# Eight more turns by blocks and a way through DRAM, in place of 64 TensorE transposes; the first such turn of the first feed-forward three units later

## What is computed

```python
# first block
x = x + 0.5 * swiglu(rmsnorm(x, ffn1_norm), ffn1_w_gu, ffn1_w_down)      # f1
h = rmsnorm(x, mix_norm)                                                # rows turned: "x"
z = h @ w_in                                   # u, v, c_q, c_kv, k_rope, q_m, gates
y_a = spatial_gating(gelu(u), gelu(v), ...)                              # turned: "a"
y_b = mla(c_q, c_kv, k_rope, positions, ...)
q = rmsnorm(q_m heads); kv = rmsnorm(mem) @ w_kv; k = rmsnorm(k heads)   # turned: "qm", "mk"
y_c = softmax(q k^T * 128 ** -0.5) v           # 4 heads of 128; turned: "c"
x = x + (g0 * (y_a @ w_a) + g1 * (y_b @ w_b) + g2 * (y_c @ w_c)) @ w_out
x = x + 0.5 * swiglu(rmsnorm(x, ffn2_norm), ...)                         # f2
# second block: gate_b, gate_c, hv = split(h2 @ conv_w_in)
u2 = gate_c * hv                               # first 512 columns turned: "uu"
x = x + gate * ((gate_b * conv3(u2)) @ conv_w_out)     # gate_b's first 512: "gb"
# ... and a third feed-forward f3, a last norm
```

## Time and profile before

| | |
|---|---|
| median of three runs | 895.51 us |
| the profiled execution | 894.65 us |
| its span, first to last instruction | 892.9 us |
| PE busy | 879.3 us, 98% of the span |
| DVE, ACT, POOL busy | 71%, 52%, 5% |
| DMA moved | 215.12 MB, 241 GB/s |
| granted PE clock, mean | 0.996 |

### The profile page before, as it was taken

One profiled execution on the slowest core, in us unless ns is written; L12 is line 12 of the kernel. 1 busy time (PEld: TensorE's weight loads), 2 busy tenths in 40 slices (PEclk: granted clock), 3 DMA queues, 4 the chain that ended last, 5 costly groups with the idle time before them and its releaser, 6 DMA issues.

```text
span 892.9 us, 11084 instructions
## 1 busy us (share of the span) xinstructions
PE 879.3 (98%) x4079; PEld 733.2 (82%) x4079; DVE 631.5 (71%) x883; ACT 460.7 (52%) x697; POOL 41.5 (5%) x66
## 2 busy tenths in 40 slices
PE   9989999999999999999999999999999999999996
PEld 7868888888988888888888888888888888888885
DVE  6669997847458867678577887775768776665743
ACT  6455644626678376546544454453545344444530
POOL 0010000013103000000000000001000100000000
PEclk9999999999999999999999999999999999999999
DMA  9889999865545454454589999974755577777831
GB/s 361 322 314 345 356 344 342 310 191 192 181 158 186 166 190 165 164 170 163 190 291 354 345 330 344 326 266 150 254 189 169 185 244 245 237 239 244 250 120 47
DMA packets 94878, 215.12 MB, mean 241 GB/s; under 512 B 14520, under 2 KB 46184, under 8 KB 94696
## 3 DMA queue, kind: packets, MB, share of 16 engines
q1 hardware_dynamic: 94104, 212.97, 69.7%
q10 hardware_dynamic: 720, 1.44, 0.4%
HBM read 204.66 MB, written 9.72 MB: 240 GB/s over the span
## 4 chain that ended last, share of the span: by engine, by line
PE 93%; DMA 2%; issue 1%; DVE 1%; SPq 1%; ACT 0%; POOL 0%; POOLq 0%; DVEq 0%
PE ps L736 29%; PE ps L738 29%; PE ps L737 29%; PE ps L674 1%; PE ps L651 1%; DMA t_raw<-in_f_up 1%; DMA t_acc<-in_c 1%; PE ps L644 1%; PE ps L853 1%; PE ps L869 1%; PE ps L811 0%; PE ps L845 0%; DMA t_acc<-in_xT 0%; PE ps L793 0%; SPq L1836 0%
## 5 line engine op out<-in xcount | busy, mean ns | idle before, releaser
L1204 DVE TENSOR_TENSOR t_wl<-t_raw,t_wh 128x1024 fp32r<-128x1024 f32 (+3 forms) x308 | 360.3, 1202 | 109.5 <-ACT t_wh L911 108.6
L911 ACT ACTIVATE t_wh<-t_raw 128x1024 fp32r<-128x1024 f32 (+3 forms) x308 | 307.8, 1040 | 116.5 <-DMA t_raw<-in_f_up 72.1
L736 PE MATMUL ps<-t_wh,t_XH 128*128 128x512 f32 (+2 forms) x640 | 250.6, 392 | 4.3 <-DVE t_wl L1204 4.3
L738 PE MATMUL ps<-t_wh,t_XL 128*128 128x512 f32 (+2 forms) x640 | 247.4, 387 | 0.0
L737 PE MATMUL ps<-t_wl,t_XH 128*128 128x512 f32 (+2 forms) x640 | 247.3, 386 | 0.0
L736 PEld LDWEIGHTS ps<-t_wh,t_XH 128*128 128x128 f32 x640 | 120.6, 188 | 27.5 <-DVE t_wl L1204 4.7
L738 PEld LDWEIGHTS ps<-t_wh,t_XL 128*128 128x128 f32 x640 | 120.5, 188 | 24.2
L737 PEld LDWEIGHTS ps<-t_wl,t_XH 128*128 128x128 f32 x640 | 120.7, 189 | 23.1
L736 PE MATMUL ps<-t_wh,t_YH 128*128 128x512 f32 x288 | 113.0, 392 | 0.2 <-DVE t_YL L1629 0.2
L738 PE MATMUL ps<-t_wh,t_YL 128*128 128x512 f32 x288 | 112.2, 389 | 0.0
L737 PE MATMUL ps<-t_wl,t_YH 128*128 128x512 f32 x288 | 112.1, 389 | 0.0
(11 more groups left out here) (225 smaller groups left out, 613.4 us busy)
## 6 DMA issues: line engine op xcount, KB each, us to landing
t_raw<-in_f_up SPq DMA_DIRECT2D x130, 512.0 KB, 5.5
t_raw<-in_f_dn SPq DMA_DIRECT2D x66, 512.0 KB, 5.1
t_raw<-in_ada SPq DMA_DIRECT2D x48, 512.0 KB, 6.0
inner_rows<-t_tp SPq DMA_DIRECT2D x60, 128.0 KB, 3.4
t_tp<-inner_rows SPq DMA_DIRECT2D x15, 512.0 KB, 5.2
...
```

The lines of the kernel that those rows point to most:

```text
L736: pe.matmul(o, xh, h, start=k == 0, stop=False)
L738: x = pe.matmul(o, xl, h, start=False, stop=k == n - 1)
L911: act.activation(wh[:, m % SPL, lo:w], raw[:, n % RAW, lo:w], ACT.Copy).then_inc(hi_made, 1)
L1204: dve.tensor_tensor(wl[:, n % RAW, lo:w], raw[:, n % RAW, lo:w], wh[:, m % SPL, lo:w].bitcast(F32), ALU.subtract).then_inc(drained, 1)
```

## The change

- Eight turns go by blocks that went by PE: the mixer's norm in two halves ("x" 0 and 1), `MK` ("mk"), `QM` ("qm"), the branches "c" and "a", and the first halves of the convolution's `UU` ("uu") and `GB` ("gb"). With them go PE's `nturn` of f1, `mem_in`, `y_turn` of c and a, and `conv_turn` and `gate_turn` of the first half: 4 + 4 + 4 + 2 + 2 groups of four transposes.
- There are three ways in place of one: `tp`, and the halves of `acc2`, with DRAM places and semaphores of their own.
- f1's first turn by blocks is spilled, reloaded and read behind units 11, 12 and 14, not 8, 9 and 12.
- `mem(n)` stands behind k = 17 + 2n, not 15 + 2n.

The core of the diff:

```diff
+            ways = (3, 4, 6) if (f, q) == ("f1", 0) else (0, 1, 3 if q == 4 else 4)
...
         if p == "f1":
-            S.extend([("scaled", p, t, j) for t in (0, 1) for j in (0, 1)])
+            for j in (0, 1):
+                S.extend([("scaled", p, 0, j), ("scaled", p, 1, j), ("blocks", "x", j)])
...
-    side = {3: [*turn(0, 0), *turn(0, 1), ("mk_stat", 0)], 5: [*turn(1, 0), *turn(1, 1), ("mk_stat", 1)],
+    side = {0: [("spill", "x", 0)], 1: [("reload", "x", 0), ("spill", "x", 1)], 2: [("reload", "x", 1)],
+            3: [("mk_stat", 0)], 4: [("xsplit", 0)], 5: [("mk_stat", 1), ("xsplit", 1)],
+            7: [("blocks", "mk")], 8: [("spill", "mk")], 9: [("reload", "mk")],
+            12: [("blocks", "qm"), ("qm_stat", 0)], 13: [("spill", "qm"), ("qm_stat", 1)], 14: [("reload", "qm")], ...
...
-        side[15 + 2 * n] = side.get(15 + 2 * n, []) + mem(n)
+        side[17 + 2 * n] = side.get(17 + 2 * n, []) + mem(n)
+    for n, br in ((32, "c"), (39, "a")):
+        for m, step in ((0, "blocks"), (1, "spill"), (2, "reload"), (5, "y_in")):
+            side[n + m] = side.get(n + m, []) + [(step, br)]
...
+        way = tp, acc2[:, 1, :], acc2[:, 0, :]
+        inner_rows = nc.dram_tensor("inner_rows", (3, 4, 8, 32, P), F32, kind="Internal").ap()
...
+            def xsplit(j):                                   # ACT
+                act.wait_ge(*is_back("x", j))
...
+                for c in range(4):
+                    k = 4 * j + c
+                    m = act.activation(by_block(XH[:, k, :]), chunk_back(c, "x", j), ACT.Copy, scale=C["mix"][:, k:k + 1])
+                m.then_inc(*x_parts_hi.by(j))
...
+                for t in (0, 1):                             # DVE, blocks of all but the feed-forwards
+                    m = dve.transpose(to[:, 512 * t:512 * t + 512].rearrange("p (j c n) -> p c j n", j=4, c=4),
+                                      rows[:, t, :].rearrange("p (c j n) -> p c j n", c=4, j=4))
```

More of the change, by code:

```diff
@@ L170, in inner @@
     def inner(f, u):
-        return [(step, f, q) for q in range(6) for step, late in (("spill", 0), ("reload", 1), ("inner", 3 if q == 4 else 4))
-                if u == (8 * q + 8 if q < 5 else 44) + late]
+        out = []
+        for q in range(6):
+            first = 8 * q + 8 if q < 5 else 44
+            ways = (3, 4, 6) if (f, q) == ("f1", 0) else (0, 1, 3 if q == 4 else 4)
+            out.extend((step, f, q) for step, late in zip(("spill", "reload", "inner"), ways) if u == first + late)
+        return out
     def ups(f, extra, head):
@@ L317, in schedule @@
             for m in range(4):
-                unit("conv_cc1", m, *([("gate_turn", 0, m), ("gate_low", 0, m)] if m < 2 else []))
+                unit("conv_cc1", m, *([("spill", "gb"), ("conv_taps", 0, 0)], [("reload", "gb"), ("conv_taps", 0, 1)], [], [])[m])
         S.append(("conv_gc", i))
         for m in range(4):
-            unit(f"conv_hv{i}", m, ahead=5)
+            unit(f"conv_hv{i}", m, *([("gate_in",), ("gate_low", 0, 0), ("gate_low", 0, 1)] if i and m == 0 else []), ahead=5)
         S.append(("conv_uu", i))
-        for m, steps in enumerate(([("conv_turn", i, 0), ("conv_turn", i, 1)], [("conv_taps", i, 0)], [("conv_taps", i, 1)], [])):
+        if i == 0:
+            S.append(("blocks", "uu"))
+            turns = [("spill", "uu")], [("reload", "uu")], [], [("ut_in",)]
+        else:
+            turns = [("conv_turn", i, 0), ("conv_turn", i, 1)], [("conv_taps", i, 0)], [("conv_taps", i, 1)], []
+        for m, steps in enumerate(turns):
             unit(f"conv_gb{i}", m, *steps, ahead=5 + (i and m // 2))
         S.append(("conv_gb", i))
+        if i == 0:
+            S.append(("blocks", "gb"))
     late("co")
@@ L512, in build @@
         inner_keys = [(f, q) for f in FFNS for q in range(6)]
-        blocked = Signal(sem("blocked"), inner_keys)
+        turned_keys = steps("blocks")
+        blocked = Signal(sem("blocked"), turned_keys)
+        spilled, reloaded = ([sem(f"{n}{w}") for w in range(3)] for n in ("spilled", "reloaded"))
+        x_parts_hi, x_parts = Signal(sem("x_parts_hi"), [(0,), (1,)]), Signal(sem("x_parts"), [(0,), (1,)])
         hid_hi, hid_lo = Signal(sem("hid_hi"), both(inner_keys)), Signal(sem("hid_lo"), both(inner_keys))
-        spilled, reloaded = sem("spilled"), sem("reloaded")
         halves = steps("half")
@@ L757, in nturn @@
             def nturn(p, t, j):
[L758 removed]
+                b = bank((p, t, j), *n_lo.at(p, t, j))
                 pe.wait_ge(*scaled.at(p, t, j))
@@ L776, in lat_turn @@
                                          src[:, t, (j + i) * P:(j + i) * P + P], ident[:, :])
-                m.then_inc(turned, 1)
-            def mem_in_(h):
-                b = bank(("mem_in", h), mqk_made, h + 1)
-                if h == 0:
-                    pe.wait_ge(*evac.at("qm", 1))
-                    pe.wait_ge(mk_made, 2)
-                for i, src in enumerate((QM, MK)):
-                    for t in (0, 1):
-                        m = pe.transpose(ps[:, b, i * 256 + t * P:i * 256 + t * P + P], src[:, t, h * P:h * P + P], ident[:, :])
                 m.then_inc(turned, 1)
@@ L1063, in mem_in_ @@
             def mem_in_(h):
[L1064 to L1065 removed]
                 if h:
                     act.wait_ge(turned, place["mem_sc", h - 1][1])
[L1068 to L1069 removed]
+                else:
+                    act.wait_ge(*is_back("mk"))
+                    act.wait_ge(*is_back("qm"))
+                act.activation(by_block(mqk[:, 0:256]), chunk_back(h, "qm"), ACT.Copy, scale=C["mqn"])
+                act.activation(by_block(mqk[:, 256:512]), chunk_back(h, "mk"), ACT.Copy, scale=C["mkn"]).then_inc(mqk_made, 1)
             def mem_exp(h):
@@ L1166, in conv_gb @@
                     if i and t == 0:
-                        act.wait_ge(turned, place["cg", 0, 1][1])
+                        act.wait_ge(*blocked.at("gb"))
                     act.wait_ge(*tile_done(f"conv_gb{i}", t))
@@ L1430, in qm_stat @@
                 if t == 0:
-                    dve.wait_ge(turned, place["f1", 1, 1][1])
+                    dve.wait_ge(*blocked.at("x", 1))
                 head_squares(QM[:, t, :], 4, mp[0], ss)
@@ L1553, in att_val @@
                 if h == 0:
-                    dve.wait_ge(turned, place["y", "a", 1][1])
+                    dve.wait_ge(*blocked.at("a"))
                 dve.wait_ge(turned, full)
@@ L1593, in conv_uu @@
                 if i:
-                    dve.wait_ge(turned, place["ut", 0, 1][1])
+                    dve.wait_ge(*blocked.at("uu"))
                 for t in (0, 1):
```

189 lines of the change are left out of this document (125 added, 64 removed), and 4 rows, old and new, of the table side.

## The result

The changed kernel takes **897.75 us** (median of 15 runs, 895.56 to 899.69) against 895.36 for the kernel before in the same comparison (15 runs, 894.09 to 896.56): a ratio of 1.0026, 95% interval 1.0018 to 1.0035. It is slower by 0.26%, where 887.4 us had been forecast. The profiled execution took 896.42 us with a span of 894.7; before, it took 894.65 with a span of 892.9.

A forecast was written before the change was run, and what follows sets the result against it. PE, busy 98% of the span, was taken as the bound; -7.0 - 6.1 + 1.3 + 3.7 = -8.1 us took the profiled 894.65 to 886.6, and the median forecast was 887.4 us, range 883.0 to 890.5.

The forecast's parts named there:

- Part 1: Transposes at f1, mixer and convolution: 64 leave PE, 0.11 us each, -7.0 us.
- Part 2: f1's hole at 52 us: with the spill three units later, unit 17's load leaves earlier; -6.1 us.
- rest of 0.7: f1: the less favourable end, where 0.7 us of waiting and the clock's 2.4 us remain.
- Part 3: Start of the mixer: x's second half returns late through DRAM and PE waits at k = 10; +1.3 us.
- x0 is in time for k = 8: Start of the mixer: x's first half has 7 us more than the second, so no wait.
- `mk` and `qm` are due at k = 19 (240) and I find them back at 238.: Mixer: the memory's turned keys and queries return before PE needs them, so no wait.
- rival 4: Start of the mixer: long serial DRAM trips for x make the kernel slower, say 898 us; chance 3%.
- Part 4: Memory attention two steps later: PE waits ahead of ukv0, ukv1, u and the first MLA transpose; +3.7 us.
- K's rows: First MLA transpose: DVE's chain of row norms ends after PE arrives, a wait of 0.9 us.
- The rest: Convolution and mixer from k = 38 on: splits stand far ahead of PE, no new wait; 0 us.
- Rival 2: Near 265 to 272 us or at k = 10: new waits lower the clock, +1.7 to +3.4 us; chance 13%.
- Rival 3: f1: the hole only moves, to the loads behind unit 13; -2.0 us in all, 893.5 us; chance 5%.

The follow-up runs named there:

- e9: Kernel before with the loads of the memory and small rows, and what is made of them, later (loads 8 units), f1's first pair unmoved; 0.9994 of the kernel before.
- e3: Changed kernel with the memory's queries and keys turned by PE and the memory attention at its old places; 0.9965 of the kernel before.
- e4: Changed kernel with the memory's queries and keys turned by PE, the memory attention still two steps later; 1.0006 of the kernel before.
- e5: Changed kernel with x turned by PE as before, without x's trip through DRAM; 0.9981 of the kernel before.
- e12: Kernel before with f1's later pair, memory by blocks and DRAM, memory attention two steps later, c's turn by PE two units later; 0.9989 of the kernel before.
- e8: Kernel before with f1's pair at 3, 5, 7, c and a by blocks at later units, convolution's first half by blocks; 0.9942 of the kernel before.
- e15: Kernel before with f1's pair at 3, 5, 7, convolution's first half by blocks, its second half's transposes and taps one unit later; 0.9938 of the kernel before.
- e6: Kernel before with only the convolution's first half (u and g) by blocks and DRAM; 0.9987 of the kernel before.

## Why the prediction was wrong, point by point

**Part 1, -7.0: right.** 4015 matmuls, and steps of -0.8 to -0.9 for each eight transposes.

**Part 2, -6.1: the hole went, the sum was 1.6 too good.** "The two loads behind unit 13 leave some 3.5 us late, at 47.5": they left at 50.24 (the spill, among full DMA engines, landed at 49.80 and took 10.9 us from its first issue), and PE wanted unit 19 at 57.4 with its weights split at 58.4. The "rest of 0.7" of the other end was the likelier one. The cause named, SP's stand, was not the whole one: e9 removes the hole although SP stands for the blocks and spills as before. And the DMA engines' 0.60 is the share of one slice, 35 to 40 us, just behind SP's stand until 35.71; from 14 to 50 us it is 0.87 before and 0.94 in the changed kernel, so there was less room than that slice suggests.

**Part 3, +1.3: measured 2.5.** The trip was right: x's second half was back at 210.70, 23.7 us after PE began the mixer (187.02), forecast 215.3 - 191.8 = 23.5. The steps behind it were mis-sized. DVE's second eight rests took 2.98 us where 2.2 were put (the first eight took 2.19), and they began at 212.46, 0.3 later than drawn:

```profile
207.00 2.19 DVE L1429 SCALAR_TENSOR_TENSOR t_XL<-t_acc,t_cols,t_XH 128x128 fp32r<-128x128 f32 x8 [6.01 <-ACT t_XH L1026]
...
212.46 2.98 DVE L1429 SCALAR_TENSOR_TENSOR t_XL<-t_acc,t_cols,t_XH 128x128 fp32r<-128x128 f32 x8 [0.60 <-ACT t_XH L1026]
```

And "x0 is in time for k = 8" missed by 0.4: its spill took from 193.43 until 200.79 to land.

**The step that failed: "`mk` and `qm` are due at k = 19 (240) and I find them back at 238."** This one line had no sum behind it, so the wait for the first scores stood at nothing in the forecast; it cost 5.2 us, 3.4 of waiting and 1.8 at the lower clock. On SP's queue v's loads stand ahead of its spill; and spill and reload took 226.96 to 239.48, 12.5 us, the length of f1's first trip (12.6), not of its second (9.1). The first scores were wanted at 237.1 and came at 240.5. It is the mechanism of rival 4 (a long trip on one queue with loads ahead of it), at a place where no rival had it. With the memory by PE the wait is gone (e3, e4), and without x's trip, whose price I had put only on x, it is 1.3 to 1.4 us with no fall of the clock (e5, e12): x's trip gives 3.7 of the 5.2.

**Part 4, the rest: +3.7, right.** With E = 255.60 in this trace, `QT`'s first tile was forecast at E + 13.7 = 269.3, and PE went on at 269.31. The wait was forecast as 2.1 and measured as 1.9; K's rows as 0.9, measured 1.0. ACT's chain is as drawn (head 3's exponential waits for DVE's maximum, which stands behind a split and a head's values):

```profile
266.13 0.60 DVE L1559 TENSOR_SCALAR t_QM<-ps,t_sc 128x128 f32<-128x128 f32 x2
266.66 0.15 DVE L1552 RECIPROCAL t_sc<-t_sc 128x2 f32<-128x2 f32 x1
266.73 0.67 DVE L1543 TENSOR_REDUCE t_sc<-ps 128x2 f32<-128x512 f32 x1
...
267.63 0.56 ACT L1126 ACTIVATE t_hn<-ps,t_sc 128x256 f32<-128x256 f32 x1 [1.41 <-DVE t_sc L1547]
```

But its cause for K's rows was only half right: e3 has that wait with the memory at its old place, and e8 hasn't with c's blocks moved. It comes with c's eight transposes leaving PE while the chain on DVE stays as long. The table load behind head 2's exponential took 1.28 us, from 259.25, and the `Gelu` followed at 260.55. The Trainium skill ("ScalarE: Activation LUTs", What ACT_TABLE_LOAD costs) adds a drain of 1.38 us to each switch; this trace does not show one either.

**The rest, 0: wrong by 2.3.** 1.5 at gc0's third unit and 0.8 in the convolution, where I had looked at the splits' lead over PE but not at what else of DVE's PE waits for (a head's maximum, `UU`).

**The rivals.** Rival 2 (the clock falls behind new waits) came true at the first scores (1.8), in e12, e4 and e15. Rival 3 came true by a quarter. The time is the 898 of rival 4, but not by its way: x's own waits are 2.5, and the loss is the sum of several places. In the mixer eight transposes cost PE 0.88 us, and by the traces x, memory and c lost more than they took; a kept 0.5 without c. In the convolution 16 by blocks gave 1.2 us (e6); there the splits stand 2.4 to 15 us ahead of PE. The Trainium skill names TensorE for a full 128x128 turn where the result may go to PSUM ("VectorE: DVE Perf Modes", Rules for kernel authors). The traces agree for x, the memory and c, and do not for the convolution.

The errors by size: first scores 5.2, f1 1.6, MLA heads 1.5, x 1.2, convolution 0.8, less 0.3 that part 4 and 0.3 that the start fell short of: 9.7 of the 9.8 us between the 886.6 forecast for the profiled execution and its 896.42. The largest is the line with no sum behind it. The median of the runs lies 1.33 above the profiled execution, where the forecast had put 0.86; this half microsecond is not explained, since only one execution was traced.
